# Ten expert slots of the last pass moved from the samples' stage into the merge and the output

## What is computed

```
xn = rmsnorm(x); z = xn @ w_in
merged = sum over branches b of sigmoid(g_b) * (y_b @ w_br_b)
x = x + merged @ w_out
# PEER, for each token: 8 heads, 16 experts each
q = xn2 @ wq; top 16 of 16 x 16 candidate key pairs per head -> experts, gates
act = gelu(xn2 . u[experts])
x = x + sum over experts of gates * act * v[experts]
```

## Time and profile before

| | |
|---|---|
| median of 3 runs | 3555.07 us (3552.26 to 3556.37) |
| the profiled execution | 3555.39 us, its span 3553.6 us |
| busy: TensorE, VectorE | 3064.8 us (86%), 2324.3 us (65%) |
| busy: GpSimd, ScalarE | 1221.6 us (34%), 1085.7 us (31%) |
| transfers | 1311.76 MB, mean 369 GB/s |
| granted TensorE clock, mean | 0.953 |
| samples' stage, merge, output | 90.9, 194.9, 59.9 us |

### The profile page before, as it was taken

The page is one execution under the profiler, slowest core; times in us unless marked ns, Lnnn a source line. Parts: engine busy times, 40 slices in busy tenths (PEclk is TensorE's granted clock), DMA queues, the critical chain, the costliest instruction groups (busy, mean ns, idle before and its releaser), DMA issues.

```text
span 3553.6 us, 31315 instructions
## 1 busy us (share of the span) xinstructions
PE 3064.8 (86%) x9822; PEld 1767.2 (50%) x9822; DVE 2324.3 (65%) x5255; ACT 1085.7 (31%) x3272; POOL 1221.6 (34%) x1043
## 2 busy tenths in 40 slices
PE   7979789989987989989987989988999798777777
PEld 4667554545655544445665644443566453322222
DVE  1331578785566778885666878886667778864444
ACT  1220243442212343442222333343221233332222
POOL 0100233343433333442343333343333325444442
PEclk9999899999998999999998999997999899999999
DMA  5334899999999999999999999998999999999998
GB/s 167 103 119 133 317 416 408 381 391 364 420 419 383 375 367 421 414 380 377 416 420 416 390 369 408 394 386 333 394 420 419 405 369 408 421 421 421 422 420 356
DMA packets 206133, 1311.76 MB, mean 369 GB/s; under 512 B 27122, under 2 KB 29242, under 8 KB 73319
## 3 DMA queue, kind: packets, MB, share of 16 engines
q0 software_dynamic: 152800, 1084.63, 75.1%
q1 hardware_dynamic: 49111, 213.07, 15.6%
q10 hardware_dynamic: 4056, 12.06, 1.0%
HBM read 1293.24 MB, written 17.61 MB: 369 GB/s over the span
## 4 chain that ended last, share of the span: by engine, by line
PE 55%; DMA 27%; DVE 9%; ACT 5%; issue 3%; POOL 1%; SPq 0%; ACTq 0%; DVEq 0%; POOLq 0%
PE ps L897 24%; DMA arena<-uv,eidx 19%; PE ps L939 10%; PE ps L1152 6%; PE ps L1114 5%; DVE arena L1561 4%; DMA wbuf<-w_merge 4%; PE ps L1118 3%; PE ps L1135 2%; DMA wbuf<-w_o 2%; DVE xx L1519 1%; PE ps L957 1%; ACT wgt L1243 1%; ACT dgs L1250 1%; DMA wbuf<-w_z 1%
## 5 line engine op out<-in xcount | busy, mean ns | idle before, releaser
L2050 POOL DMA_INDIRECT arena<-uv,eidx x1032 | 1205.8, 1168 | 2148.3 <-PE ps L897 1598.5
L897 PE MATMUL ps<-arena,dgs 128*128 128x512 f32 x3196 | 1544.5, 626 | 291.5 <-ACT dgs L1250 275.3
L1561 DVE CUSTOM_DVE_ANT_0 arena<-arena,xx 128x1024 f32<-128x1024 f32 x1024 | 1238.6, 1222 | 622.0 <-DMA arena<-uv,eidx 594.4
L897 PEld LDWEIGHTS ps<-arena,dgs 128*128 128x128 f32 x3196 | 614.2, 199 | 1043.1 <-issue 616.1
L1231 ACT ACTIVATE gel<-dots 128x2 f32<-128x2 f32 x516 | 104.3, 202 | 1391.8 <-DVE dots L1561 1391.3
L939 PE MATMUL ps<-wbuf,xT 128*128 128x420 f32 (+1 forms) x1152 | 427.1, 520 | 13.1 <-DMA wbuf<-w_z 12.2
L1519 DVE SCALAR_TENSOR_TENSOR xx<-arena,wgt,xx 128x1024 f32<-128x1024 f32 x225 | 288.3, 1281 | 55.2 <-ACT wgt L1243 52.6
L1114 PE MATMUL ps<-xT,wbuf 128*128 128x256 f32 (+1 forms) x1344 | 312.5, 386 | 12.1 <-DMA wbuf<-w_merge 10.6
L939 PEld LDWEIGHTS ps<-wbuf,xT 128*128 128x128 f32 (+1 forms) x1152 | 204.6, 180 | 235.6 <-issue 220.4
L1114 PEld LDWEIGHTS ps<-xT,wbuf 128*128 128x128 f32 x1344 | 256.2, 192 | 79.0 <-DMA wbuf<-w_merge 27.9
L1250 ACT ACTIVATE dgs<-cst,wgt 128x128 f32<-128x128 f32 x799 | 286.9, 396 | 15.9
(11 more groups left out here) (367 smaller groups left out, 1981.2 us busy)
## 6 DMA issues: line engine op xcount, KB each, us to landing
wbuf<-w_merge SPq DMA_DIRECT2D x84, 768.0 KB, 8.5
wbuf<-w_z SPq DMA_DIRECT2D x64, 840.0 KB, 8.8
wbuf<-w_q SPq DMA_DIRECT2D x64, 512.0 KB, 7.8
arena<-uv,eidx POOLq DMA_INDIRECT x1032, 12.3
wbuf<-w_o SPq DMA_DIRECT2D x32, 512.0 KB, 7.8
xin<-x_prompt SPq DMA_DIRECT2D x8, 1024.0 KB, 12.7
wbuf<-w_merge SPq DMA_DIRECT2D x12, 512.0 KB, 8.2
grow<-gains SPq DMA_DIRECT2D x8, 512.0 KB, 10.8
```

The costliest lines, as they stand in the source:

```text
L897: done = mm(ps[:, half, :], dgs[:, j, :], ring[:, j, row_], start=(q == 0), stop=(q == P - 1), skip_group_check=True)
L1561: v.tensor_tensor_reduce(ring[:, j, 0:D], ring[:, j, 0:D], x, 1.0, 0.0, ALU.mult, ALU.add, dots[:, j:j + 1]).then_inc(s["dotted"], 1)
L2050: g.indirect_dma_start(ring[:, j, :], None, uv, bass.IndirectOffsetOnAxis(ap=experts, axis=0)).then_inc(got[j], 16)
```

## The change

The shares of the last pass are changed: the samples' stage carries 14 slots instead of 24, the merge 66 instead of 60, the output 24 instead of 20. The sums agree, so nothing before the samples' stage and nothing behind the output is different, and the same 1032 slots are computed.

```diff
-    (... ("b", 46), ("x", 24), ("m", 60), ("o", 20), ("n1", 4), ...),
+    (... ("b", 46), ("x", 14), ("m", 66), ("o", 24), ("n1", 4), ...),
```

## The result

The change makes the kernel slower by about 14 us: 3566.99 us (median of 16 runs, 3557.82 to 3577.09) against 3552.73 (16 runs, 3543.04 to 3568.48), ratio 1.0041 with a 95% interval of 1.0030 to 1.0052. The forecast was 3563.3. The profiled execution of the changed kernel took 3570.06 us.

What follows compares the result with a forecast made beforehand. Transfers without a gap were taken to bound merge and output, a latency chain the samples' stage. The terms -11.1 + 17.5 - 1.5 + 3 gave +7.9 us on 3555.39, so 3563.3 us, range 3551 to 3573.

Steps and rivals of the forecast that it cites:

- What bounds the kernel: Merge and output are bound by transfers, 2.50 us a slot; the samples' stage is a chain with DMA time to spare.
- (a): Samples' stage: ten slots fewer on TensorE save 11.1 us, bounds 4.1 and 17.9, of at most 23.7.
- (b): Merge's start: seven more gathers still to move, +17.5 us; the reload of the prompt's rows already through, -1.5 us.
- (e): Residual's load, now issued in the merge's first point: costs 0, at most 2 us, since VectorE has idle time.
- signs that I had named: Profile after: merge starts at 2510.5, 12 us or more longer; output near 70; samples' DMA share near 0.8, clock at most 0.81.
- (c): Merge's start: a new gap in transfers until the first slot is freed, +3 us, bounds 0 and 6.
- a sign of being wrong: Stages behind the output differing by more than 3 us would show the prediction wrong.
- the walk: Samples' stage: chain of rounds, dots, slots and fills followed step by step; merge's first matmul at 2510.5 instead of 2521.6.
- (d): Six slots in the merge, four in the output: TensorE's and VectorE's work stays hidden behind transfers, costing nothing.
- the rival of VectorE as the output's bound: Output: VectorE, planned at 91%, can't use its idle time; up to 8 us on top, 3571.3 us; chance 0.10.
- all of TensorE's time comes back: Samples' stage: state rounds wait only for TensorE, 23.7 us come off, 3550.7 us in all; chance 0.22.
- merge and output hide the gathers: Merge and output: the ten gathers cost nothing, only the saving stays, 3544.3 us; chance 0.06.

Runs made afterwards that it cites:

- e7: The changed kernel, with the last pass's merge loading only seven eighths of each weight tile, all instructions else the same: 3559.42 us, ratio 1.0026.
- e5: Against the kernel before: ten slots go from the samples' stage (14) to the tail's end (162), merge and output as before: 3565.28 us, ratio 1.0036.
- a2: The changed kernel, nothing altered, run once more for a second profile: 3566.64 us, one run.
- e8: The changed kernel, with the six slots that it moved from TensorE to VectorE given back to TensorE: 3568.07 us, ratio 1.0052.
- e1: Against the kernel before: six slots go from the samples' stage (18) to the merge (66), output stays at 20: 3557.80 us, ratio 1.0017.
- e11: Against the kernel before: 28 slots in the samples' stage instead of 24, merge 58, output 18: 3561.90 us, ratio 1.0023.
- e4: Against the kernel before: 34 slots in the samples' stage instead of 24, merge 54, output 16: 3559.04 us, ratio 1.0022.

## Why the prediction was right, and where its terms were off

**What bounds the kernel** held: merge and output at a share of 1.01 before and after, e7's eighth of the weights, and the tail's 2.3 to 2.6 us a slot in e5. The forecast was +7.9 us and a range of 3551 to 3573; it came to +14.3 in the medians (+14.7 between the two profiled executions), within the range, on the side that had the larger chance. That it lies inside is owed in part to the width of the range: 6.8 us of the 14.7 were missed, with (a), (b) and (e) off the same way.

Of the signs that I had named, the merge's start (2511.27), its +12.4 us, the output's 70.2 us and the clock (0.69) came as said. The samples' stage's DMA share is 0.69 and not near 0.8, and the merge runs at 414 GB/s and not 420, for the gap of (c). The tail is 3.5 us longer, more than the 3 that I had called a sign of being wrong; that bound was too tight, since the same code took 606.2 to 610.9 us in the other traces.

**(a), the samples' stage, was mis-sized**: 11.1 us saved by the walk, bounds 4.1 to 17.9, and 6.8 in the trace (6.7 in a2 against before's first profile). The chain is the one that I walked: rounds at 2463.5, 2473.2, 2484.6 and 2495.0 in the trace, 2464.4, 2473.0, 2483.3 and 2493.5 in the walk, and the merge's first matmul at 2511.27 against 2510.5. But this execution's stage began 3.5 us earlier, and counted from its start the walk, 79.8 us, is 4.3 too short. The term that was mis-sized is the clock in that chain. I carried fills of 3.7 us and pairs of 5.4 into a stage with two empty points, and named fills and pairs at the low clock only as the bound. They were what happened: a fill of 7.1, in all five traces without additions, and pairs of 6.66, 6.44 and 5.88. Of the 4.3 us, 2.6 were lost before round 0, where half of a run of four slots (4.3 us in the walk) was a pair of 6.66 and fill 0 took 4.6 for 3.6. Fill 1 itself cost 1.1, VectorE's wait for it, the pair of 6.44 another 1.1, and the rest of the chain was 0.5 shorter. Where the clock rose earlier, in e7 and e8, the stage is 79.7 and 80.1 us, the length of the walk, though by luck in part, since their fill 1 took 7.1 us as well. e1, at 18 slots with no empty point, has a clock of 0.77 and 82.4 us, within the 79.7 to 84.7 of 14 slots.

**(b), what is left at the merge's start**: seven gathers predicted, 17.5 us, and -1.5 for the reload. Merge and output moved 7.98 MB more of gathers, 7.6 gathers or 19.0 us at 420 GB/s; SyncE's queue moved 17.92 MB in the merge where it was

```profile
q1 hardware_dynamic: 3551, 18.74, 23.3%
```

before, -0.82 MB or -2.0 us.

**(c), the gap**: 3 us predicted. The merge's first 20 us and the next:

```profile
2511.30:2531.30 20.00, 20.00 (x73) 13.56 (x72) 8.49 (x17) 4.10 (x15) 6.50 (x6) 1.00 0.96 364
2531.30:2551.30 20.00, 19.32 (x76) 13.91 (x75) 14.39 (x21) 4.00 (x15) 7.99 (x8) 1.00 1.01 408
2551.30:2571.30 20.00, 19.15 (x72) 13.18 (x70) 12.89 (x20) 5.29 (x19) 6.29 (x7) 1.00 1.01 422
```

At 364 and 408 GB/s instead of 420, 2.7 and 0.6 us are lost: 3.3. TensorE is busy for all of the first 20 us, and GpSimd waits for the places that it frees, at the longest 3.6 us (until 2516.98).

**(d), engines hidden in merge and output**, held, with less to spare than I said. The output is at 1.01 and 419 GB/s with VectorE at 60.8 of 70.2 us, so the rival of VectorE as the output's bound fell. e8 shows that the merge's first 60 us had no room on TensorE for the four of the six slots that lie there.

**(e), the residual's load**, was priced for its latency alone, at nothing. It has bytes as well: 0.52 MB that moved in the samples' stage before now move in the merge (q10 above), 1.2 us at 420 GB/s. Of a moved step I had counted the issue and not the size.

**The sum, mended**: -6.8 for the stage, +19.0 for gathers, -2.0 for the reload, +1.2 for the residual and +3.3 for the gap give +14.7, and the three stages of the traces differ by +14.7. For merge and output this had to come out nearly so, since bytes over rate is their length; what it shows is how many bytes moved there, and at which rate.

**The rivals.** That all of TensorE's time comes back is out: 6.8 us of 23.7. That merge and output hide the gathers is out: +21.5 us. That rival rested on a sentence in the Trainium skill ("Perfetto Trace Analysis", "Optimizing DMA Performance", "Optimization Strategies"), to keep the matmul engine as busy as possible; this case doesn't test that advice, since TensorE's busy share fell with the change, in the samples' stage from 88 to 81% and in the merge from 95.6 to 94.5%. What falls is the rival's premise, a merge that waits for TensorE: e7 leaves TensorE's instructions as they are, loads fewer bytes, and the merge is shorter.

**What stays open**: whether e11's hole in the merge belongs to its edit, why e4's output starts at 311 GB/s, and what sets in which places of the samples' stage the clock is low in a given execution.

## What to carry to other kernels

Work whose transfers are hidden in a stage bound by latency costs that stage less than their transfer time, and moved to a stage at full DMA share it costs about its bytes: here 1.3 to 1.8 us a slot above 18 slots in the one, 2.3 to 2.6 in the others. The way back doesn't pay by itself: with 28 and 34 slots in the samples' stage the kernel was 6 us slower too, in part because the ring freed its places too late for all of the added gathers to move there. Make the ledger in bytes that still have to move when the bound stage starts, with every small load that moves along, not in instructions. And before emptying a stage of TensorE's filling work, price the rest of its chain at the low clock as well: the filling work may be what keeps it high.

## What the chip showed that I had not expected

- With less work on TensorE the same work took longer: slots at 2.37 us each at a mean granted clock of 0.81, and 2.83 at 0.69. Fill 1, four matmuls of 512 columns with 8 rows of weights, two records each, behind a wait of 2.6 us, took 7.1 us at a granted clock of 0.50, the 1.2 GHz level, where fill 0 and the later ones took 3.7 to 4.8; two records are 1.91 us there and 1.02 at 2.4 GHz.
- The same instruction stream got its clock back at different places: the pair behind the score matmuls took 6.66, 6.71 and 6.56 us in three traces and 3.70 in two (granted clock 0.54 in after, 1.00 in e7).
- One core moved 420 GB/s for 209 us on end (e1's merge), with two kinds of traffic, row gathers of 8 KB and weights. The Trainium skill ("DMA: Bandwidth & Descriptors", "Where 436 GB/s comes from") says that for transfers from HBM a limit near 358 GB/s binds, half of what two cores share, and names 425 GB/s measured for 16 MB. For this kernel's one core the row agrees with the second figure, and the first did not bind.
